# VectorE's order in the blocks with gate matrices: weights' low half, one-hots, fetched row; rows two blocks later

## Reference

```
expert = take_along_axis(cand_idx, pos)          # 8 heads x 16 picks = 128 per token
gate = softmax(best)
ub, vb = u_tab[expert], v_tab[expert]
a = gelu(einsum('td,ted->te', xb, ub))
y = einsum('te,ted->td', gate * a, vb)
```

## Time and profile before

| quantity | value |
|---|---|
| time, median of 3 executions | 2172.92 us (2167.83 to 2175.38) |
| span of the profiled execution (first to last instruction) | 2161.6 us |
| time of the profiled execution beside its span | not recorded; the median of the timed ones is 11.3 us above this span |
| PE busy | 98% of the span |
| DVE, ACT, POOL busy | 67%, 40%, 48% |
| mean granted TensorE clock | 0.996 of full speed |

### The profile page before, as it was taken

One profiled execution on the slowest core, in us unless ns is written; L12 is line 12 of the kernel. 1 busy time (PEld: TensorE's weight loads), 2 busy tenths in 40 slices (PEclk: granted clock), 3 DMA queues, 4 the chain that ended last, 5 costly groups with the idle time before them and its releaser, 6 DMA issues.

```text
span 2161.6 us, 29125 instructions
## 1 busy us (share of the span) xinstructions
PE 2121.7 (98%) x10648; PEld 1837.8 (85%) x10648; DVE 1442.4 (67%) x2713; ACT 858.3 (40%) x1306; POOL 1038.6 (48%) x573
## 2 busy tenths in 40 slices
PE   8989999999999999999999999999999999999999
PEld 7857888888877877899999999999998888888887
DVE  5973411110054995369998777787867999999987
ACT  4354522232264454253334444444433333333332
POOL 1203244443423333435566888888863444444342
PEclk9999999999999999999999999999999999999999
DMA  4202344444442222334347899998899999999996
GB/s 177 82 27 62 104 117 127 117 119 115 117 118 74 86 71 77 117 106 121 112 147 207 242 267 321 284 315 249 261 309 318 388 388 371 373 375 377 369 359 251
DMA packets 240489, 444.14 MB, mean 205 GB/s; under 512 B 102459, under 2 KB 152028, under 8 KB 240220
## 3 DMA queue, kind: packets, MB, share of 16 engines
q1 hardware_dynamic: 152060, 299.07, 41.8%
q0 software_dynamic: 55488, 134.83, 19.3%
q10 hardware_dynamic: 32800, 8.39, 1.8%
HBM read 397.71 MB, written 44.50 MB: 205 GB/s over the span
## 4 chain that ended last, share of the span: by engine, by line
PE 69%; POOL 13%; DVE 8%; issue 4%; DMA 3%; ACT 2%; SPq 0%; DVEq 0%; ACTq 0%; POOLq 0%
PE bank L469 22%; PE bank L473 22%; PE bank L472 22%; POOL gate_matrices L1151 9%; POOL y L1160 4%; DMA y<-in_peer_u_rows,gidx 3%; DVE m L1979 1%; PE bank L923 1%; DVE xn L1980 1%; DVE WL L2297 1%; PE bank L645 1%; DMA wraw<-in_peer_u 1%; ACT sc L1302 1%; DVE y L2308 0%; DVE hots L2329 0%
## 5 line engine op out<-in xcount | busy, mean ns | idle before, releaser
L1140 POOL TENSOR_TENSOR WL<-wraw,WH 128x1024 fp32r<-128x1024 f32 x171 | 435.9, 2552 | 723.5 <-ACT WH L1191 723.5
L1191 ACT ACTIVATE WH<-wraw 128x1024 fp32r<-128x1024 f32 x411 | 435.0, 1060 | 627.4 <-PE bank L469 393.6
L469 PE MATMUL bank<-XH,WH 128*128 128x384 f32 (+2 forms) x1864 | 668.8, 359 | 12.6 <-DVE WL L2297 7.8
L473 PE MATMUL bank<-XH,WL 128*128 128x384 f32 (+2 forms) x1864 | 657.8, 353 | 0.0
L472 PE MATMUL bank<-XL,WH 128*128 128x384 f32 (+2 forms) x1864 | 657.6, 353 | 0.0
L469 PEld LDWEIGHTS bank<-XH,WH 128*128 128x128 f32 x1864 | 351.4, 189 | 46.3 <-issue 12.9
L472 PEld LDWEIGHTS bank<-XL,WH 128*128 128x128 f32 x1864 | 351.6, 189 | 29.0 <-issue 0.7
L473 PEld LDWEIGHTS bank<-XH,WL 128*128 128x128 f32 x1864 | 351.1, 188 | 28.7
L2297 DVE TENSOR_TENSOR WL<-wraw,WH 128x1024 fp32r<-128x1024 f32 x240 | 293.0, 1222 | 57.6 <-ACT WH L1191 51.8
L469 PE MATMUL bank<-WH,GH 128*128 128x512 f32 x768 | 298.9, 389 | 1.6 <-issue 1.6
L473 PE MATMUL bank<-WH,GL 128*128 128x512 f32 x768 | 298.8, 389 | 0.0
(11 more groups left out here) (313 smaller groups left out, 2561.8 us busy)
## 6 DMA issues: line engine op xcount, KB each, us to landing
wraw<-in_peer_u SPq DMA_DIRECT2D x128, 512.0 KB
wraw<-in_peer_v SPq DMA_DIRECT2D x128, 512.0 KB
activations<-ac SPq DMA_DIRECT2D x122, 192.0 KB
ar<-activations SPq DMA_DIRECT2D x122, 192.0 KB
gr<-gate_matrices SPq DMA_DIRECT2D x124, 128.0 KB
wraw<-in_w_gate SPq DMA_DIRECT2D x22, 512.0 KB
wraw<-in_w_up SPq DMA_DIRECT2D x22, 512.0 KB
wraw<-in_w_down SPq DMA_DIRECT2D x22, 512.0 KB
```

Source lines behind the costliest of these rows:

```text
L469: mm = pe.matmul(out, wh, xh, start=first, stop=False)
L473: return pe.matmul(out, wl, xh, start=False, stop=last)
L1140: pool.tensor_tensor(WL[:, u % NW, 0:m], wraw[:, u % NR, 0:m], WH[:, u % NW, 0:m].bitcast(F32), ALU.subtract).then_inc(s("w_lo"), 1)
L1191: act.activation(WH[:, u % NW, 0:k * n], wraw[:, u % NR, 0:k * n], ACT.Copy).then_inc(s("w_hi"), 1)
```

## Change

Three things are changed in the DVE program and none on another engine. The two rows that were used ahead of the loop are no longer used there. In an iteration the low half comes first, then the one-hots, then the rows. And `rows_until` gives slot n in the gate-matrix blocks n rows where it gave n+2; the two missing rows are added in slots 86 and 87, which use two rows each, so that from slot 88 on the numbers are the old ones.

```
-EARLY = 2
+BEHIND = 2
...
-    rest = 2 * HS - EARLY - ups
-    return EARLY + after + min(max(slot - ups, 0) * rest // (NEXP - 4), rest)
+    rest = 2 * HS - BEHIND - ups
+    return min(max(slot - GATE_UPS, 0), BEHIND) + after + min(max(slot - ups, 0) * rest // (NEXP - 4), rest)
...
                 hots_of(FIRST_GATE_UP)
                 low(LOW_BY_DVE + 1)
-                for row in range(EARLY):
-                    use_row(row)
                 for x in range(FIRST_GATE_UP, NEXP):
+                    low(unit_at[("u", x)] + 2)
                     hots_of(x + 1)
                     use_rows(x - FIRST_GATE_UP)
-                    low(unit_at[("u", x)] + 2)
```

## The result

The changed kernel takes 2155.1 us in the median of six executions (2154.0 to 2158.3), the kernel before 2168.3 us in the median of six (the three known ones among them). The ratio is 0.9938, 95% interval 0.9921 to 0.9955: 13 us faster. The forecast was 2170.3 us, with 0.20 for faster by more than 0.3%. The time lies outside the range (2164.5 to 2176.0), and the gain is five times the one that was worked out.

The account below looks back on a forecast made before the run. PE was taken to wait for rows fetched at POOL's pace, through DVE's order. Winning 6.9 us, less 1.4 (block 123), 1.7 (clock) and 1.2 (loop's end), gave 2.6: 2172.9 - 2.6 = 2170.3 us, range 2164.5 to 2176.

Parts of the forecast that it names:

- What bounds the kernel: In the gate-matrix stage PE waits for fetched rows through DVE's order; low-half waits in the up blocks total 7.0 us.
- Low half first, 6.9 us up to block 119: PE's four waits up to block 118 go: 5.2 us, with the slow clock 6.9 us.
- One-hots behind the low half, 0: Making one-hots after the low half in an iteration still meets their due time: cost 0, bounded by 0 and 3 us.
- POOL's pace is unchanged: From row 0 to row 88 POOL still takes 427.6 us, 4.86 a row; bounds 7 us either way.
- row 89 did not hold block 123: Forecast said the opposite: at the catching up in slots 86 and 87, PE waits until 1607.4, losing 1.4 us.
- 1.7 us of slow clock: Ahead of block 123, 3.6 us of PE idling was expected to lower the clock again, costing 1.7 us.
- rival B: Row 89 does not hold PE at block 123: 5.7 us won, 2167.2 us; chance 0.23.
- The copy of unit 123 moves along: ACT's copy still ends 17.7 us after block 119 began, at 1604.6, so the row decides and not the copy.
- The end of the loop, 1.2 us: Row 96's use falls between the last low half and the first weighing, adding 1.2 us before the down blocks.
- The comparison with the median: The median lies 11.3 us above the profiled span; that was carried over unchanged to the forecast.
- Rival C: PE stays tied to POOL in the stage, late rows still holding low halves: 2172 to 2173 us; chance 0.12.
- rival D: POOL's stretching grows with the new phase, at the fetch of row 89: 7 us more gives 2177.3 us; chance 0.15.

Follow-up runs that it names:

- halved scatters: Every second scatter left out on POOL, in both kernels: kernel before 2155.6 us (ratio 0.9947), changed kernel 2155.2 us (0.9935).
- memsets: One small POOL memset added behind each fetch of rows 0 to 87, in both kernels: kernel before 2180.4 us, changed kernel 2168.1 us.
- changed twice: The changed kernel's two profiled runs, the second with no edit: medians 2155.1 us (ratio 0.9938) and 2155.7 us (0.9941).
- distance only: Changed kernel with rows used two blocks later but the old order in the loop (one-hots, row, low half): 2155.7 us, ratio 0.9938.
- one behind: Changed kernel with half the distance, one row used ahead of the loop and the new order kept: 2154.7 us, ratio 0.9930.
- first weighings: Changed kernel with the use of row 96 moved behind the first two weighings and the first weighted low half: 2154.3 us, ratio 0.9932.
- order only: Changed kernel's loop order (low half, one-hots, row), with two rows used ahead of the loop as in the kernel before: 2168.3 us, ratio 0.9990.
- slowed changed: Changed kernel with a small POOL memset behind each fetch of rows 0 to 87: 2168.1 us, ratio 1.0007 to the kernel before.
- slowed before: Kernel before with a small POOL memset behind each fetch of rows 0 to 87: 2180.4 us, ratio 1.0052.
- second profile of the kernel before: Kernel before run again with no edit: median 2168.9 us, ratio 0.9996; the profiled execution took 2163.8 us.
- third profile of the kernel before: Kernel before profiled again with no edit: this execution took 2168.1 us.

## Why the prediction was wrong

*What bounds the kernel*: right. PE waited for rows through DVE's order, and the rows came at POOL's pace. The halved scatters (2155.6 us with nothing changed on DVE) and the memsets (12 us, with row 88 11 to 15 us later) show it from both sides.

*Low half first, 6.9 us up to block 119*: right in size (7.3 in the first pair of profiles), wrong in its cause. I gave the gain to the order in the iteration. The order alone gives nothing, the distance alone gives all of it.

*One-hots behind the low half, 0*: 0.46 us of waiting in the profile, ahead of the first group.

*POOL's pace is unchanged*: this is the step that failed. I took 427.6 us up to row 88 and no change "since DVE does the same instructions". With rows behind, POOL takes 415 to 419 us, waits for DVE included, in five profiles (changed twice, distance only, one behind, first weighings). Its scatters and fetches fill 338 us from row 0 to row 88 in both profiles of the changed kernel and 360 to 364 in the four of the kernel before. I had named the phase of DVE against POOL, and even priced it at 7 us either way, but put it under "slower"; and I had POOL wait for nothing, where it waited 15.9 us for row buffers. So row 89 did not hold block 123: 16.7 us from block 119, where my sum had 20.5, and the 1.7 us of slow clock behind it were not paid. From there come some 5.5 us more than forecast. It is rival B, which had 0.23.

*The copy of unit 123 moves along*: wrong as well, and needed for the same 5.5 us. I had it end 17.7 us after block 119 began, which would have made PE wait there even with row 89 in time, as distance only shows (copy at 17.6, 19.0 us from block 119). So of the 3.8 us between 20.5 and 16.7 about 1.5 are the row's and 2.3 the copy's, which ended after 13.6. No run shows by itself why its load landed sooner. (Also, half of the 8.57 us is 4.3 us a block and not the 4.2 that I wrote; the changed kernel took 4.2.)

*The end of the loop, 1.2 us*: wrong. I followed DVE's queue and not ACT's; the cost was 0, with ACT's copy as the cover. (From block 123 to the first down block the changed kernel still takes 0.7 us more, 0.5 of it a wait for the low half of block 125.)

*The comparison with the median*: wrong by more than any of these. I carried 11.3 us around the span from one execution to the median; some 2 us lie around it. Of the other 9.3, 4.6 are the median itself, which was 2172.9 us for the three known executions and is 2168.3 for six, and 4.7 are what the ordinary execution of that median takes longer than the profiled, quick one; by the two later profiles that is mostly waiting for rows. With it the miss adds up: the forecast was 15.2 us too high, 9.3 from this, 6.4 from the stretch between block 33 and the down blocks (9.0 us won instead of 2.6), and 0.5 the other way.

The quick executions also say how the change is to be counted. From block 33 to the down blocks the kernel before takes 465 and 466 us in its quick ones and 471 and 472 in the two near the median, the changed kernel 455 and 456. The quick pair alone gives 9 us for the change, the ordinary executions 15 to 17, and the means of four and of two profiles 12.8, beside the 13 measured. No execution of the kernel before beyond 2172 us was profiled, so its slowest (to 2178) are unseen.

Rival C (still tied) is what order only does, and rival D (POOL slower) what the memsets do. Left open is how much of the gain needs POOL's shorter instructions: every kernel with rows behind has both the distance and the shorter instructions, except the slowed changed one, which kept the stage free of waits and paid at the catching up. Also open is why a scatter takes 1.94 to 1.96 us in some executions of the kernel before and 1.90 to 1.92 in others.

## What to carry to other kernels

In a loop on an in-order engine, turning the order inside an iteration does not take a late arrival off the path; it only changes whom it holds first. What helps is the distance between an arrival and the first work that stands behind it, and one iteration more was enough here. When two engines run at nearly one pace (4.86 and 4.85 us), treat each execution's waits as a draw, take several profiles before making a sum, and read the chain on the profile's page for an engine that should not be in it.

## What the runs showed of the hardware

POOL's indirect-DMA instructions take 1.00 us (fetch) or 1.58 us (scatter), unless a DVE instruction is under way when they start; then they last longer by about what is left of it, less 0.13 us. POOL in the changed kernel, 1299 to 1310 us:

```profile
1299.14 2.53 POOL L1151 DMA_INDIRECT gate_matrices<-scat_gate,scat_at  x1 [0.30 <-issue]
1301.98 1.55 POOL L1151 DMA_INDIRECT gate_matrices<-scat_gate,scat_at  x1 [0.30 <-issue]
...
1307.82 1.84 POOL L1160 DMA_INDIRECT y<-in_peer_u_rows,gidx  x1 [0.30 <-issue]
1309.96 1.59 POOL L1151 DMA_INDIRECT gate_matrices<-scat_gate,scat_at  x1 [0.30 <-issue]
```

and DVE beside it:

```profile
1299.01 1.21 DVE L2329 TENSOR_TENSOR hots<-iota,sq 128x1024 f32<-128x1024 f32 x1
...
1300.87 1.22 DVE L2308 CUSTOM_DVE_ANT_0 y<-y,x_nat 128x1024 f32<-128x1024 f32 x1
...
1307.55 1.23 DVE L2297 TENSOR_TENSOR WL<-wraw,WH 128x1024 fp32r<-128x1024 f32 x1 [2.79 <-ACT WH L1191]
...
1309.95 0.73 DVE L2333 TENSOR_TENSOR hots<-hots,rt 128x512 f32<-128x512 f32 x1
```

The scatter at 1299.14 starts when 1.08 us of DVE's L2329 are left and takes 2.53, the fetch at 1307.82 when 0.96 of a low half are left and takes 1.84, the one at 1301.98 when 0.11 us of a row are left and takes 1.55. The one at 1309.96 starts 0.01 us after L2333 and takes 1.59: where both start together, POOL's keeps its length and DVE's is a little longer (0.73 us here, 0.69 alone). In the 14 profiles of this study none of more than 200 starts within 0.02 us of each other lengthened POOL's instruction, and the DVE instruction took 1.25 to 1.30 us instead of 1.22, or 0.70 to 0.75 instead of 0.69. A DVE instruction that begins while one of POOL's is already running keeps its length.

L2333 looks like an exception and is none. Nearly all of the 354 starts under it fall on its first 0.03 us or its last 0.14, where little or nothing is to be had. The four in between were 0.33 to 0.45 us longer. One of them, in the third profile of the kernel before, starts with 0.51 us of L2333 left and takes 1.98 us instead of 1.58:

```profile
1221.62 1.98 POOL L1151 DMA_INDIRECT gate_matrices<-scat_gate,scat_at  x1 [0.50 <-DMA gate_matrices<-scat_gate,scat_at]
```

```profile
1221.44 0.69 DVE L2333 TENSOR_TENSOR hots<-hots,rt 128x512 f32<-128x512 f32 x1
```

Worked out from the timelines between rows 0 and 88: in the first profile of the kernel before, 125 of 217 POOL instructions start under a low half, a row or L2329, and 70 us are stretching; in the changed kernel it is 104 of 217 and 48 us. The tied kernels (before in four profiles, order only, slowed before) have 70 to 79 us, the untied ones (changed twice, distance only, one behind, first weighings) 42 to 52, and the slowed changed kernel, in which DVE waits 41 us for rows, 70. So being tied goes together with a slower POOL, and a slower POOL keeps PE tied. A reason would be that DVE's three instructions then start when POOL's row lands and not when ACT's copy is done; that is argued and no run shows it by itself.

The Trainium skill ("SBUF — State Buffer", "Who interferes with whom") says that a DVE instruction with two SBUF inputs contends with a GpSimd instruction that reads SBUF, and that "Issue order, not op shape, decides who blocks." The trace agrees on both, for low half, row, L2329 and L2333, though what DVE lost where it was not first was never more than 0.08 us.

How long PE idled did not say alone whether the clock fell. Behind 2.38 us of idling it was 0.58 for 4 us, behind 2.80 us in the second profile of the kernel before 0.57, behind 4.76 us in the slowed changed kernel 0.61. Behind 2.98 us in the third profile of the kernel before it stayed at 1.00, and behind 3.4 us in order only (PE goes on at 1617.3, ahead of block 123) too:

```profile
1617.00:1621.00 4.00, 3.65 (x21) 3.68 (x22) 3.62 (x6) 0.11 (x1) 2.80 (x3) 1.00 1.02 404
```

So the 1.7 us that I charged for a second fall of the clock were a possible cost and not a sure one.
